# A hybrid S5, mLSTM and attention trunk on one core: row maxima broadcast by one product of high and low rows, GpSimd held behind VectorE's splits, Toeplitz blocks cleared in parts

## What is computed

```python
def mlstm_chunkwise(q, k, v, i_pre, f_pre):
    log_f = jax.nn.log_sigmoid(to_chunks(f_pre)); log_i = to_chunks(i_pre)
    b = jnp.cumsum(log_f, axis=-1)
    ...
    d_log = jnp.where(causal, b[..., :, None] - b[..., None, :] + log_i[..., None, :], -jnp.inf)
    m_t = jnp.maximum(inter_log, d_log.max(-1))
    w_intra = jnp.exp(d_log - m_t[..., None]) * jnp.einsum('bhctd,bhcsd->bhcts', q, k)
    num = einsum(w_intra, v) + ...
    h = num / jnp.maximum(jnp.abs(den), jnp.exp(-m_t))[..., None]

def s5_group(u, ...):
    _, states = lax.associative_scan(_linear_recurrence_combine, (a_seq, bu), axis=1)
    y = einsum(states.real, c_re) - einsum(states.imag, c_im) + d_skip * u
    g = gelu(y);  return g * sigmoid(g @ w_glu)
```

## Time and profile before

| what | before |
|---|---|
| median of 3 runs | 1081.69 us (1081.07 to 1082.23) |
| profiled execution, its own time | 1083.43 us |
| its span | 1081.6 us |
| PE busy | 1068.1 us (99%) |
| DVE / ACT / POOL busy | 639.7 / 463.8 / 188.1 us |

### The profile page before, as it was taken

One profiled execution on the slowest core, in us unless ns is written; L12 is line 12 of the kernel. 1 busy time (PEld: TensorE's weight loads), 2 busy tenths in 40 slices (PEclk: granted clock), 3 DMA queues, 4 the chain that ended last, 5 costly groups with the idle time before them and its releaser, 6 DMA issues.

```text
span 1081.6 us, 15533 instructions
## 1 busy us (share of the span) xinstructions
PE 1068.1 (99%) x5556; PEld 865.7 (80%) x5556; DVE 639.7 (59%) x874; ACT 463.8 (43%) x732; POOL 188.1 (17%) x243
## 2 busy tenths in 40 slices
PE   9999999999999999999999999999999999999997
PEld 7887578888888888888888777888888888888886
DVE  6799754566666666633334775656666666643332
ACT  6455565444434343422233565553444344422221
POOL 8999720400000000000000222310000000000000
PEclk9999999999999999999999999999999999999998
DMA  6551024232222222222324111223222222222322
GB/s 228 166 126 41 20 84 175 78 117 98 97 97 97 97 97 97 97 98 99 108 94 156 60 51 50 98 97 99 96 97 97 97 97 97 97 98 97 117 78 78
DMA packets 36459, 107.27 MB, mean 99 GB/s; under 512 B 7808, under 2 KB 10112, under 8 KB 36160
## 3 DMA queue, kind: packets, MB, share of 16 engines
q1 hardware_dynamic: 36416, 106.69, 29.7%
HBM read 102.09 MB, written 3.15 MB: 97 GB/s over the span
## 4 chain that ended last, share of the span: by engine, by line
PE 88%; DVE 2%; issue 1%; POOL 0%; ACT 0%; DVEq 0%
PE bank L1569 28%; PE bank L1570 27%; PE bank L1571 27%; PE bank L1593 1%; PE bank L1957 1%; PE bank L1934 1%; PE bank L1779 1%; PE bank L1714 1%; DVE wlo L1037 1%; PE bank L1707 0%; PE bank L1742 0%; PE bank L1736 0%; POOL pbuf L670 0%; DVE outb L1540 0%; DVE wbuf L1226 0%
## 5 line engine op out<-in xcount | busy, mean ns | idle before, releaser
L1569 PE MATMUL bank<-xhi,whi 128*128 128x512 f32 x960 | 376.5, 392 | 0.1
L1570 PE MATMUL bank<-xlo,whi 128*128 128x512 f32 x960 | 373.8, 389 | 0.0
L1571 PE MATMUL bank<-xhi,wlo 128*128 128x512 f32 x960 | 373.7, 389 | 0.0
L1037 DVE TENSOR_TENSOR wlo<-raw,whi 128x1024 fp32r<-128x1024 f32 x177 | 233.4, 1320 | 209.2 <-ACT whi L687 208.7
L687 ACT ACTIVATE whi<-raw 128x1024 fp32r<-128x1024 f32 x177 | 187.0, 1057 | 327.2 <-PE bank L1571 304.8
L1569 PEld LDWEIGHTS bank<-xhi,whi 128*128 128x128 f32 x960 | 180.3, 188 | 39.4 <-issue 0.8
L1571 PEld LDWEIGHTS bank<-xhi,wlo 128*128 128x128 f32 x960 | 180.3, 188 | 37.9
L1570 PEld LDWEIGHTS bank<-xlo,whi 128*128 128x128 f32 x960 | 180.4, 188 | 37.2 <-issue 0.3
L1569 PE MATMUL bank<-ahi,whi 128*128 128x512 f32 (+1 forms) x374 | 142.4, 381 | 0.0
L1570 PE MATMUL bank<-alo,whi 128*128 128x512 f32 (+1 forms) x374 | 142.2, 380 | 0.0
L1571 PE MATMUL bank<-ahi,wlo 128*128 128x512 f32 (+1 forms) x374 | 142.2, 380 | 0.0
(11 more groups left out here) (258 smaller groups left out, 1057.4 us busy)
## 6 DMA issues: line engine op xcount, KB each, us to landing
raw<-wstream SPq DMA_DIRECT2D x177, 512.0 KB, 3.2
xin<-xT SPq DMA_DIRECT2D x8, 256.0 KB, 5.4
raw<-wstream SPq DMA_DIRECT2D x8, 256.0 KB, 5.0
h<-xT SPq DMA_DIRECT2D x1, 2048.0 KB, 8.5
u_scratch<-uperm SPq DMA_DIRECT2D x1, 1024.0 KB, 5.5
uc<-u_scratch SPq DMA_DIRECT2D x8, 128.0 KB, 4.9
bandsb<-band SPq DMA_DIRECT2D x1, 1024.0 KB, 4.8
outT<-outb SPq DMA_DIRECT2D x2, 512.0 KB, 2.9
```

Source lines behind the costliest of these rows:

```text
L1037: V.tensor_tensor(wlo[:, t % RING, :], raw[:, t % RAWS, :], whi[:, t % RING, :].bitcast(f32), ALU.subtract).then_inc(lo_done, 1)
L1569: MM(dst, wh, rhi, start=start, stop=False)
L1570: MM(dst, wh, rlo, start=False, stop=False)
L1571: return MM(dst, wl, rhi, start=False, stop=stop)
```

## The change

- At the start, DVE instead of ACT makes the high part of the very first half tile, and PE waits for `first_hi`.
- POOL waits, before it turns the first half of the S5 inputs, until DVE has made the splits of tiles 15 and 16 (`lo_done` of 17). In the second turn back it waits after `tprod` until DVE has made `head_sum(0)`.
- The skip term is added to `ksb` directly behind its copy; `out_gate(1)` moves from behind the row chain into it; `turned_half(0)` and `(1)` stand ahead of the copy of `acol`; `turned_half(2)`, `(3)` and `out_gate(3)` stand ahead of `weights(1)`.
- The row maxima get a high part (rows 0 to 3 of `nm`) and a low part (rows 32 to 35), both fp32r. The broadcast is one fp32r product, 36 rows deep, with a selector `selr`. `nm` is cleared by POOL, `selr` copied by ACT.
- On PE `head_scores(0)` no longer waits for `acol`, and `head_scores(1)` stands behind `project(T_O + 3)`.
- `toep` is cleared in parts: blocks 4 and 5 by ACT (behind the exponentials of head 1), 6 and 7, then 0 to 3, by POOL. SP copies blocks 5, 4, 7, 6, 3, 2, 1, 0 in that order.
- In the loop over heads, `head_sum` stands ahead of a weights step and `mask_decay` behind it, and the split of tile 18 moves from hd = 1 to hd = 2.

```diff
@@ sync
-        sp.wait_ge(toep_clear, 1)
-        for t in range(CH):
-            sp.dma_start(toep[(CH - 1 - t) * GCH:P, t, :, :],
-                         ksb[0:(t + 1) * GCH, :, :]).then_inc(toep_built, 16)
+        for ts, free, need in (((5, 4), toep_mid, 1), ((7, 6), toep_clear, 1), ((3, 2, 1, 0), toep_clear, 2)):
+            sp.wait_ge(free, need)
+            for t in ts:
+                sp.dma_start(toep[(CH - 1 - t) * GCH:P, t, :, :],
+                             ksb[0:(t + 1) * GCH, :, :]).then_inc(toep_built, 16)
@@ gpsimd
+        G.memset(nm[:, :].bitcast(f32), 0.0).then_inc(nm_clear, 1)
...
+            if after_sum:
+                pool.wait_ge(hms_added, after_sum)
...
+        pool.wait_ge(lo_done, T_QK + RING + 1)
         for b in range(2):
             turned_by(xr[:, b], part[b], True).then_inc(turned, 1)
...
-        G.memset(toep[:, :, :, :], 0.0).then_inc(toep_clear, 1)
+        G.memset(toep[:, 6:8, :, :], 0.0).then_inc(toep_clear, 1)
+        G.memset(toep[:, 0:4, :, :], 0.0).then_inc(toep_clear, 1)
@@ scalar
+        A(selr[0:32 + HEADS, :], cols("selg", 32 + HEADS)[:, 0:HEADS], ACT.Copy).then_inc(sel_set, 1)
...
+            if hd == 0:
+                act.wait_ge(scan_done, 1)
+                A(toep[:, 4:6, :, :], ones[...], ACT.Copy, scale=0.0).then_inc(toep_mid, 1)
@@ vector
+        dve.wait_ge(half_in[0], 16)
+        V.tensor_copy(whi[:, 0, 0:512], raw[:, 0, 0:512]).then_inc(first_hi, 1)
...
-        V.tensor_scalar(nmrow[:, :], peak, -1.0, None, ALU.mult).then_inc(rows_done, 1)
+        steps.up(V.tensor_scalar(nm[0:HEADS, :], peak, -1.0, None, ALU.mult))
+        settle()
+        V.scalar_tensor_tensor(out=nm[f_rows, :], in0=peak, scalar=-1.0, in1=nm[0:HEADS, :].bitcast(f32),
+                               op0=ALU.mult, op1=ALU.subtract).then_inc(rows_done, 1)
...
-            head_sum(hd - 1)
-            weights(SB * hd + 2)
             head_scale(hd - 1)
             weights(SB * hd + 3)
-            if hd == 1:
-                split_lo(T_O + hd + RING)
             if hd + 1 < HEADS:
                 weights(SB * (hd + 1))
+            if hd == 2:
+                split_lo(T_O + 1 + RING)
             head_gate(hd - 1)
@@ tensor
-            MM(bank[2][:, :], ident[0:HEADS, hd:hd + 1].to_broadcast([HEADS, P]), nmrow[:, :],
+            MM(bank[2][:, :], selr[0:32 + HEADS, hd:hd + 1].to_broadcast([32 + HEADS, P]), nm[:, :],
                start=True, stop=True).then_inc(nmb_ready, 1)
...
-        pe.wait_ge(acol_copied, 1)
         head_scores(0)
+        project(T_O + 3, O_O + 3)
+        pe.wait_ge(acol_copied, 1)
         head_scores(1)
-        project(T_O + 3, O_O + 3)
```

More of the change, by code:

```diff
@@ L228, in build @@
     cdiag = at("cdiag", [P, 2, PAIRS, 2, GCH], sigo_at + 4096)
-    nmrow = at("nmrow", [HEADS, SEQ], ssum_at - 4096)
+    nm = at("nm", [32 + HEADS, SEQ], ssum_at - 4096, f32r)
     g8 = at("g8", [104, SEQ], ssum_at)
     tail = sigo_at + 8192 + size([P, 2, PAIRS, NCH]) + 2048
-    bcp, xpad, cacc, xcf, ptmp, sm, qq, acol, turn, floor, hsm = plan(
+    bcp, xpad, cacc, xcf, ptmp, sm, qq, acol, turn, floor, hsm, selr = plan(
         ("bcp", [P, 4, PAIRS * GCH], f32), ("xpad", [P, 3 + SEQ], f32), ("cacc", [P, SEQ], f32),
@@ L236, in build @@
         ("qq", [P, 2, SUP, 2 * PAIRS], f32), ("acol", [P, SB, HEADS], f32),
-        ("turn", [P, 2, PAIRS, HALF_CH], f32), ("floor", [P, SB, HEADS], f32), ("hsm", [P, 2, 3, SB], f32), start=tail)
+        ("turn", [P, 2, PAIRS, HALF_CH], f32), ("floor", [P, SB, HEADS], f32), ("hsm", [P, 2, 3, SB], f32), ("selr", [P, HEADS], f32r), start=tail)
     pt_at = tail + 4096 + 2112 + 2 * 2048
@@ L310, in build @@
     radius_done, radius_set, min_done = sem("radius_done"), sem("radius_set"), sem("min_done")
[L311 removed]
+    nm_clear, sel_set = sem("nm_clear"), sem("sel_set")
+    arow_done, toep_mid = sem("arow_done"), sem("toep_mid")
     turned, turned_scan, carry_done, skip_set = (sem(n) for n in (
@@ L626, in _, with turned_by @@
                         ALU.mult).then_inc(skip_set, 1)
-        def turned_by(dst, src, back):
+        def turned_by(dst, src, back, after_sum=0):
             tt(tprod[:, :, :, :], src, turn[:, 0:1, :, :].to_broadcast([P, 2, PAIRS, HALF_CH]), ALU.mult)
+            if after_sum:
+                pool.wait_ge(hms_added, after_sum)
             tt(uprod[:, :, :, :], src, turn[:, 1:2, :, :].to_broadcast([P, 2, PAIRS, HALF_CH]), ALU.mult)
@@ L653, in _ @@
                 pool.wait_ge(lo_done, T_O + RING + 1)
-            turned_by(part[b], xr[:, b], False).then_inc(scan_done, 1)
+            turned_by(part[b], xr[:, b], False, after_sum=b).then_inc(scan_done, 1)
             pool.wait_ge(scan_done, b + 1)
             settle()
-        G.memset(toep[:, :, :, :], 0.0).then_inc(toep_clear, 1)
+        G.memset(toep[:, 6:8, :, :], 0.0).then_inc(toep_clear, 1)
+        G.memset(toep[:, 0:4, :, :], 0.0).then_inc(toep_clear, 1)
         for hd in range(HEADS - 1):
@@ L732, in _ @@
             act.wait_ge(raw_in[t % RAWS] if k % 2 else half_in[t], 16 * (t // RAWS + 1) if k % 2 else 16)
-            A(whi[:, t, part], raw[:, t % RAWS, part], ACT.Copy).then_inc(hi_done if k % 2 else half_hi, 1)
+            if k:
+                A(whi[:, t, part], raw[:, t % RAWS, part], ACT.Copy).then_inc(hi_done if k % 2 else half_hi, 1)
         for m in range(KB):
@@ L876, in _ @@
                     decay(hd + 1, s)
+            if hd == 0:
+                act.wait_ge(scan_done, 1)
+                A(toep[:, 4:6, :, :], ones[:, 0:GCH].unsqueeze(1).unsqueeze(1).to_broadcast([P, 2, GROUPS, GCH]), ACT.Copy,
+                  scale=0.0).then_inc(toep_mid, 1)
             if hd >= 2:
@@ L1194, in _ @@
         dve.wait_ge(kt_ready, 1)
-        V.tensor_copy(ksb[:, :, :], bank[6][:, :].rearrange("p (g i) -> p g i", i=GCH)).then_inc(k_copied, 1)
+        k_rows = bank[6][:, :].rearrange("p (g i) -> p g i", i=GCH)
+        V.tensor_copy(ksb[:, :, :], k_rows).then_inc(k_copied, 1)
+        dve.wait_ge(k_copied, 1)
+        dve.wait_ge(skip_set, 1)
+        V.tensor_tensor(ksb[0:GCH, :, :], k_rows[0:GCH], skipb[:, :].rearrange("p (g i) -> p g i", i=GCH),
+                        ALU.add).then_inc(k_final, 1)
+        dve.wait_ge(nm_clear, 1)
         dve.wait_ge(lnf_done, 1)
         dve.wait_ge(vtok_copied, HEADS)
-        lf_p, a_p, peak = bank[7][f_rows, :], bank[7][0:HEADS, :], bank[5][0:HEADS, :]
+        lf_p, a_p, peak = bank[7][f_rows, :], bank[7][0:HEADS, :], bank[6][0:HEADS, :]
         V.scalar_tensor_tensor(out=lf_p, in0=bank[0][f_rows, :], scalar=0.0, in1=lf,
@@ L1203, in _ @@
                                       ALU.mult, ALU.add))
+        out_gate(1)
         settle()
@@ L1270, in _ @@
         mask_decay(0)
[L1271 to L1276, removed]
         out_gate(2)
@@ L1279, in _ @@
         turned_half(2)
+        turned_half(3)
+        out_gate(3)
         weights(1)
-        out_gate(3)
         weights(2)
-        turned_half(3)
         mask_decay(1)
@@ L1290, in _ @@
             head_floor(hd - 1)
+            head_sum(hd - 1)
+            weights(SB * hd + 2)
             if hd + 1 < HEADS:
                 mask_decay(hd + 1)
-            head_sum(hd - 1)
-            weights(SB * hd + 2)
             head_scale(hd - 1)
             weights(SB * hd + 3)
-            if hd == 1:
-                split_lo(T_O + hd + RING)
             if hd + 1 < HEADS:
                 weights(SB * (hd + 1))
+            if hd == 2:
+                split_lo(T_O + 1 + RING)
             head_gate(hd - 1)
@@ L1700, in _ @@
         for s in range(SB):
-            ins = transpose(bank[4][:, s * HEADS:(s + 1) * HEADS], arow[:, s * P:(s + 1) * P], HEADS)
+            ins = transpose(bank[5][:, s * HEADS:(s + 1) * HEADS], arow[:, s * P:(s + 1) * P], HEADS)
         ins.then_inc(acol_ready, 1)
@@ L1759, in _ @@
         broadcast_max(0)
+        head_scores(0)
+        project(T_O + 3, O_O + 3)
         pe.wait_ge(acol_copied, 1)
-        head_scores(0)
         head_scores(1)
-        project(T_O + 3, O_O + 3)
         pe.wait_ge(k_copied, 1)
```

13 lines of the change are left out of this document (8 added, 5 removed).

## The result

| what | before | after |
|---|---|---|
| median, 7 runs each | 1081.76 us (1081.07 to 1083.66) | 1084.84 us (1082.96 to 1085.44) |
| ratio | | 1.0028, 95% interval 1.0019 to 1.0038 |
| profiled execution | 1083.43 us, span 1081.6 | 1082.96 us, span 1081.2 |

The kernel became slower by 3.1 us, or 0.28%. The prediction had 1079.2, with 1077.0 to 1081.9 as its range, so it was wrong in sign and range. The two profiled executions alone would have said the opposite (-0.47 us): the one of before is among that kernel's slowest, the one of after is the fastest of its seven. Three executions of the later runs (1178.67 and 2748.16 us of before, 2740.59 us of the kernel with one clear) were in another, slow state and are counted nowhere.

The account below looks back on a forecast made before the run. PE, busy 99% of the span, was taken to bound the kernel. Start -0.3, earlier S5 output -3.5 and clock fall +1.3 gave -2.5: median 1081.69 to 1079.2 us, range 1077.0 to 1081.9.

Parts of the forecast that it names:

- The start: First product: with DVE making the first high part, PE starts 0.15 to 0.5 us earlier, taken as 0.3.
- the two splits and the row chain: Holding POOL ends both splits near 98.8, maxima ready at 109.9; PE's 1.42 us wait and the 1.7 us clock fall go.
- the broadcast: Broadcast of the maxima on PE: start to next product 0.4 instead of 1.05 us, saving 0.65 on each of four.
- to the first value sums: PE's first value sums start at 118.8 instead of 122.58, less 1.42, 0.65 and 1.7 us.
- the heads: First value sums to S5 output: 25.1 us shrinks to 21.2, up to 1 put back; PE ready at 140.8.
- the timed executions before had no fall at 113.5: Rival: only the profiled execution had that clock fall, so 1.7 of the gain is absent: -0.8, 1080.9 us; chance 0.20.
- The warning: Profiled execution of before lies 1.74 us above the median, just the price of one fall of the clock.
- The Toeplitz copies, now late: SP's eight copies run 137.3 to 144.1 (6.8 us); PE waits 3.4, starting the S5 output 3.5 us earlier than 147.66.
- The clock again: Behind the 3.4 us wait ahead of the S5 output PE's clock falls, losing 0 to 1.7 us, taken as 1.3.
- Clearing in parts brings nothing: Clearing toep in parts gains nothing: the old clear ended at 138.8, the new one is done by 135.
- its own bounds: Bounds the forecast gave its summed median of 1079.2 us: 1077.9 to 1080.6.

Follow-up runs that it names:

- the kernel with one clear: Changed kernel with toep cleared by one POOL memset: 1081.11 us with the split of tile 18 back at hd = 1, 1085.01 us with it late.
- the run with the split late alone: Kernel before with only the split of tile 18 moved to the end of hd = 2: 1088.70 us, ratio 1.0063.
- the second profile: Another profiled execution of an unedited kernel: changed kernel 1085.22 us (third profile 1085.30), kernel before 1081.18 us (third profile 1081.39).
- the run with products in the wait: Changed kernel with 20 products of ones (128 x 128) on PE in the wait ahead of the S5 output: 1082.40 us.
- the kernels with the split back: Changed kernel with the split of tile 18 back at hd = 1: 1077.02 us; also with the copies ahead of the load of tile 20: 1077.31 us.
- the run with no load ahead of its copies: Changed kernel, split late, copies ahead of the load of tile 20 but held until the split of tile 18: 1081.92 us.

## Why the prediction was wrong

Two steps failed. The row chain was priced against waits that the usual execution does not have, and the Toeplitz copies were given too little time; the second turned the sign.

**The start, the two splits and the row chain, the broadcast, to the first value sums, the heads.** Each instruction came as written: 0.32 for 0.3, splits 2.6 for 2.4, maxima at 109.92 for 109.9, 0.43 for 0.4, value sums at 118.72 for 118.8, PE ready for the S5 output at 140.4 for 140.8. But what they were worth was taken against a profile that was not the usual one. In the usual execution PE waits for no broadcast and has no fall at 113.5, so POOL's wait brings 0, not 3.1 us (1.42 and 1.7). The start was read off one execution too: the four profiles in which ACT makes the first high part begin at 5.67, 5.77, 5.82 and 5.99, and eleven of the twelve in which DVE makes it at 5.54 to 5.79 (one at 6.51), so 0.1 or 0.2 of the 0.3 is left. The rival "the timed executions before had no fall at 113.5" was true of the base, was given 0.20, and missed that the wait itself was absent as well. The warning was in the numbers shown: the profile lay 1.7 us above the median.

The Trainium skill (SBUF — State Buffer, section "SBUF: two separate sides") says that whoever starts first holds the shared port for its whole instruction. The prediction set this aside on the evidence of one trace. By that rule the pair takes 4.8 us, an estimate. The profiles at 4.5 and 5.05 come near it; the ones at 8.68 and 8.67 (the run with the split late alone) do not. Both happen, and the median follows the first.

**The Toeplitz copies, now late.** This step found the mechanism and the place, and it was the step that decided. The copies began when it said (136.83 for 137.3), and two sizes were off. The copies were given 6.8 us, their time behind a load that had long landed; with it right ahead of them they took 8.5 and 9.8. So PE waits 5.0 to 6.2 us, not 3.4. And the gain of 3.5 was counted from 147.66, where the usual execution starts at 145.5. From there the step is not -3.5 but +1.5 (146.99 in the second profile).

**The clock again.** Taken at 1.3, with 0 to 1.7 as its bounds; it cost 1.8 in the first profile (10.60 against 8.81), 2.4 in the second (11.17), 1.5 in the third (10.26), and 2.4 by the run with products in the wait. The low stretch lasts 6.8 us, twice the one of the earlier trace rows from which the bound was taken.

**"Clearing in parts brings nothing"** holds for this kernel (1085.01 against 1084.84) and hides what the edit is worth, 4.1 us. Its reason was misread: 138.8, where the old clear ended, is behind the 137.3 at which the copies were to begin. It holds because even one clear ends at 135.79 in the changed kernel, ahead of the split of tile 18 at 136.94, which the load of tile 20 and the copies have to await anyway.

The lower end of "its own bounds", 1077.9, doesn't follow from its terms either: -0.3 - 4.5 + 0 gives 1076.9. The measured time lies far on the other side.

The sum, remade against usual executions (second profile after, third before): to the first value sums 119.95 to 119.15, -0.8; heads until PE is ready 25.55 to 21.62, -3.9; the wait +6.2; the S5 output 8.81 to 11.17, +2.4; together +3.9. Measured between the same two: 1085.22 - 1081.39 = +3.8 (+3.1 between the medians). The forecast of -2.5 misses by 6.3: 2.2 for the base, 2.8 for the wait, 1.1 for the clock, 0.2 for the rest. Without the error in the base the prediction would still have missed: the copies and the clock alone make 3.9 of it.

## What to carry to other kernels

Where a profiled execution lies off the median by as much as one of your terms, take a second profile before you cost anything against it: a wait that is in one profile may be in one execution of ten. When a split or any other step that frees a buffer is moved later, follow the queue: what stood behind the load that it released moves too, and copies that are needed soon belong ahead of a load that the bottleneck doesn't need yet. Here that alone, the changed kernel with its copies ahead of the load of tile 20, gives 1076.74 us, 8.1 under the changed kernel; the kernels with the split back are within 0.6 us of it.

## What the runs showed of the hardware

- One pair of DVE splits beside two POOL products of 1024 columns has at least two outcomes in the same program: 4.5 to 5.05 us for DVE with 2.9 to 3.4 for each of POOL's products, or 8.7 us for DVE with 2.35 and 2.38. In the second the first split, which began ahead of POOL, is the one of 6.45 us. What tips it was not found. In the five profiles of kernels in which POOL doesn't wait for the splits, its first product starts 0.67 and 0.65 us behind the first split where the pair is long, and 0.62, 0.58 and 0.53 where it is short; that is too few to call it the cause.
- A fall of the clock does not follow from the wait alone. Waits of 0.55 and 0.79 us preceded one at 131 in the second profile of the kernel before, nearly the same waits (0.55, 0.80) none in the third; a wait of 2.73 us was followed by none in the profile with one clear, one of 3.29 by a fall.
- A fall can be nearly free. The second profile of before has PE at 0.50 from 131 to about 134.3 and 1.3 us of waits for `wbuf`; the third has 1.00 and 2.6 us of such waits. From the first value sums to the S5 output they take 25.87 and 25.55 us. Here most of the slow products' extra time falls where PE would have waited for DVE.
- Eight copies took longer with a load of 512 KB issued just ahead of them on the same queue. The window from 138 to 140, in the changed kernel and then in the run with no load ahead of its copies (columns as above):

```profile
138.00:140.00 2.00, 1.71 (x16) 1.52 (x15) 1.24 (x4) 0.88 (x3) 1.01 (x1) 1.00 1.00 335
...
138.00:140.00 2.00, 1.70 (x13) 1.51 (x13) 1.68 (x6) 0.93 (x3) 0.71 (x2) 1.00 0.80 253
```

  With both under way the DMA share is 1.00, with the copies alone 0.80, and the copies take 1.3 to 2.6 us less without the load ahead of them (7.2 against 8.5 and 9.8).
